# The opening of a hybrid trunk kernel: norm rows spread by TensorE, sample rows in one transfer, bands finished on GpSimd, differences between a group's two weight chunks

## The chip, the cores and the metric

The kernel runs on one core of a Trainium2 chip. The metric is the device time of one execution in microseconds, lower is better. 0.2% of it is 5.0 us.

## What is computed

One step of a two-layer decoder trunk in float32 over 320 tokens (256 of a new prompt, 8 sequences of 8 new tokens each) with 2048 features. Layer 0 mixes by pooling, layer 1 by an mLSTM; a squared-ReLU MLP follows each. The change is in the opening, the pooling mixer of layer 0:

```python
u = rmsnorm(h, norm_mix[layer])
def pool_mixer(u, buf, pos0, w_group, scale):
    u_ext = jnp.concatenate([buf, u], axis=1)          # buf: the last 15 inputs of each sequence
    cs = jnp.cumsum(jnp.pad(u_ext, ((0, 0), (1, 0), (0, 0))), axis=1)
    for g, w in enumerate((2, 4, 8, 16)):              # four groups of 512 features
        s = cs[:, P + 1:P + 1 + T, sl] - cs[:, P + 1 - w:P + 1 - w + T, sl]
        outs.append(s / cnt[None, :, None])            # mean of the last w inputs
    d = (pooled - u_ext[:, P:]).reshape(B, T, 4, 512)
    y = jnp.einsum('btgc,gcd->btgd', d, w_group) * scale
    new_buf = u_ext[:, T:]
h = h + y
h = h + sq_relu_mlp(rmsnorm(h, norm_ffn[layer]), ...)
```

## The kernel before

**The main loops.** Activations lie with features on the partitions and the 320 tokens as columns (hT is the residual, 16 tiles of 128 features). A float32 product is made of three faster ones: operand and weight are each split into a high part (`w_hi`, `a_hi`, `op_hi`, copies by ScalarE, ACT) and a low part (`w_lo`, `a_lo`, `op_lo`, by VectorE, DVE), and TensorE (PE) adds hi·hi, lo·hi and hi·lo in the accumulator G (L1600 to L1602). Weights come in chunks of 128x1024 (512 KB) through a ring of four buffers. A chunk is 24 matmuls of 320 columns. Eight chunks make a slab of 512 output features; slab 0 is the first of the MLP. After a slab, DVE takes its four tiles out of G (`relu`, L1263) and ACT and GpSimd (POOL) square and split them. Each engine has its own queue of instructions, in the order of the code, with waits on semaphores.

**The opening.** Rows of x lie with tokens on the partitions in `xrow` (two prompt tiles of 128, and a tile of 64 sample rows followed by the young state rows). ACT squares and sums each row (L869, one instruction of 2048 columns), DVE and ACT make 1/rms of it (`rcol`). POOL draws for each group g a matrix `band` (memsets L605 and L607, selects L593 and L622) of 1/w where a token counts; DVE multiplies it by `rcol` and takes the identity off (L1190, L1191, L1185). The samples are scaled by `rcol` and by the norm's row `gain` (L1198; `gain` comes in three transfers of repeated rows, `mix_rows`). Then `differences(g)` is 24 rows of matmul on PE (L1631; each float32 matmul shows as two rows): X = xrow times band is d with features on the partitions. ACT and DVE split X into `a_hi` and `a_lo` (L896, L897, L1212, L1214), and two chunks of the pooling weight (L835 and L1129 split them) give the group's output, which DVE adds to hT (L1251, "the evictions"). Group 3 has extra products with `far` (L1638). The order on PE is differences(0), differences(1), chunks 0 and 1, differences(2), chunks 2 and 3, differences(3), chunks 4 and 5, chunks 6 and 7, then the MLP's slab 0. Between the early pieces PE multiplies the identity (`keep_warm`, L1621), whose output nobody reads.

For the MLP's norm ACT squares each tile of hT into `sqt` (L912), one buffer, and POOL adds it to `acc` (L670), 16 times. PE sums `acc` over partitions in slab 0, DVE makes the reciprocal `rv`.

**POOL's list** is: the four draws; then a block of small constants that the mLSTM needs much later (`one`, `causal`, `causal_s`, `parts`, `seqmask`, `fold`, L628 to L649, and two small transfers, L652 and L653), "the constants block"; then the 16 additions to `acc`; then "the tail", which scales the last 32 prompt rows for the output new_buf (L674, L676, 32x2048 each) and sends them out; then the MLP's part.

## Time and profile before

| | |
|---|---|
| time, median of 3 runs | 2481.77 us (2481.02 to 2482.14) |
| time of the profiled execution | 2481.15 us |
| its span | 2479.4 us |
| mean granted clock of TensorE | 0.995 |
| busy share of PE, DVE, ACT, POOL | 99%, 49%, 37%, 20% |
| first matmul of the pooling weights | 27.16 us |
| first matmul of the MLP | 69.00 us |

The span runs from the first to the last instruction; the execution's time is 1.75 us longer. PE is busy in 99% of it, so only what PE waits for, or does at a low clock, can be won without taking work from it. The opening is the first 69 us.

### The profile page before, as it was taken

What the parts mean: (1) busy time and instruction counts of PE and PEld (TensorE: products, weight loads), DVE (VectorE), ACT (ScalarE), POOL (GpSimd) and SP (SyncE); (2) the same over time, 40 slices, a digit from 0 to 9 for tenths busy, and PEclk for the clock granted to TensorE, in tenths of its full rate; (3) what the DMA queues carried; (4) which work ended last, traced back from release to release, by engine and by line L of the source; (5) the groups of instructions that cost most, each with busy time, mean ns of one, the idle gap of its engine ahead of it and who ended that gap; (6) DMA issues with size and microseconds to landing.
All of it is one profiled execution on the core that took longest, in us unless ns stands there. A gap on an engine that the chain in (4) does not pass through costs nothing.

```text
span 2479.4 us, 43406 instructions
## 1 busy us (share of the span) xinstructions
PE 2452.6 (99%) x16344; PEld 2406.8 (97%) x16344; DVE 1207.4 (49%) x1391; ACT 907.2 (37%) x1075; POOL 488.3 (20%) x612
## 2 busy tenths in 40 slices
PE   8999999999999999999999999999999999999998
PEld 8999999999999999999888889999999999999997
DVE  6644344444444454444478885444344444434444
ACT  5433333233333333333355553333333233333332
POOL 5430022012102332210011122221022003101331
PEclk8999999999999999999999999999999999999999
DMA  7544444455444444555377664444454454444443
GB/s 226 153 147 153 147 150 151 146 152 147 150 151 145 151 148 134 145 145 154 107 231 225 228 208 154 149 148 153 145 151 148 148 152 145 151 150 147 152 146 113
DMA packets 197684, 387.22 MB, mean 156 GB/s; under 512 B 12181, under 2 KB 12181, under 8 KB 197173
## 3 DMA queue, kind: packets, MB, share of 16 engines
q1 hardware_dynamic: 197228, 385.46, 49.9%
q0 software_dynamic: 384, 0.78, 0.2%
q8 instruction: 48, 0.79, 0.1%
q14 instruction: 24, 0.20, 0.0%
HBM read 364.01 MB, written 22.64 MB: 156 GB/s over the span
## 4 chain that ended last, share of the span: by engine, by line
PE 95%; DVE 3%; DMA 1%; ACT 0%; issue 0%; SPq 0%; POOL 0%; DVEq 0%; ACTq 0%; POOLq 0%
PE G L1600 30%; PE G L1601 29%; PE G L1602 29%; PE X L1869 1%; PE X L1832 1%; DMA w_raw<-in_pool_w 1%; DVE w_lo L1129 0%; PE X L1631 0%; DMA w_raw<-in_mlstm_w_out 0%; DVE cst L1517 0%; PE X L1876 0%; DVE qkv L1410 0%; PE G L1910 0%; PE G L1912 0%; PE G L1914 0%
## 5 line engine op out<-in xcount | busy, mean ns | idle before, releaser
L1129 DVE TENSOR_TENSOR w_lo<-w_raw,w_hi 128x1024 fp32r<-128x1024 f32 x648 | 833.4, 1288 | 1175.0 <-ACT w_hi L821 1164.5
L821 ACT ACTIVATE w_hi<-w_raw 128x1024 fp32r<-128x1024 f32 x608 | 645.2, 1062 | 1306.2 <-PE G L1602 1275.4
L1600 PE MATMUL G<-op_hi,w_hi 128*128 128x320 f32 x2816 | 876.1, 311 | 0.7 <-DVE qkv L1319 0.7
L1602 PE MATMUL G<-op_hi,w_lo 128*128 128x320 f32 x2816 | 870.8, 309 | 0.0
L1601 PE MATMUL G<-op_lo,w_hi 128*128 128x320 f32 x2816 | 870.7, 309 | 0.0
L1600 PE MATMUL G<-a_hi,w_hi 128*128 128x320 f32 x2304 | 714.6, 310 | 4.3 <-DVE hT L1251 2.7
L1601 PE MATMUL G<-a_lo,w_hi 128*128 128x320 f32 x2304 | 713.6, 310 | 0.0
L1602 PE MATMUL G<-a_hi,w_lo 128*128 128x320 f32 x2304 | 713.4, 310 | 0.0
L1600 PEld LDWEIGHTS G<-op_hi,w_hi 128*128 128x128 f32 x2816 | 529.0, 188 | 8.2 <-issue 5.7
L1601 PEld LDWEIGHTS G<-op_lo,w_hi 128*128 128x128 f32 x2816 | 529.1, 188 | 2.4 <-issue 1.0
L1602 PEld LDWEIGHTS G<-op_hi,w_lo 128*128 128x128 f32 x2816 | 529.1, 188 | 0.0
L1600 PEld LDWEIGHTS G<-a_hi,w_hi 128*128 128x128 f32 x2304 | 433.7, 188 | 5.0 <-issue 3.3
L1601 PEld LDWEIGHTS G<-a_lo,w_hi 128*128 128x128 f32 x2304 | 433.7, 188 | 0.1
L1602 PEld LDWEIGHTS G<-a_hi,w_lo 128*128 128x128 f32 x2304 | 433.6, 188 | 0.0
L693 POOL TENSOR_TENSOR sq<-relu 128x320 f32<-128x320 f32 x128 | 120.7, 943 | 1268.4 <-DVE relu L1263 1268.3
L696 POOL TENSOR_TENSOR a_lo<-sq,a_hi 128x320 f32 x128 | 144.7, 1130 | 25.9 <-POOL sq L693 19.6
L662 POOL TENSOR_TENSOR sqt<-hT 128x320 f32<-128x320 f32 x44 | 44.4, 1008 | 178.1 <-DVE hT L1280 116.2
L918 ACT ACTIVATE a_hi<-relu 128x320 f32 (+1 forms) x128 | 55.5, 473 | 59.7 <-DVE relu L1263 59.3
L1263 DVE SCALAR_TENSOR_TENSOR relu<-G,Rb 128x320 f32<-128x320 f32 x128 | 56.6, 485 | 1.8 <-PE G L1602 1.8
L829 ACT ACTIVATE w_hi<-w_raw 128x1024 fp32r<-128x1024 f32 x32 | 33.9, 1059 | 60.8 <-DMA w_raw<-in_mlstm_w_in 32.8
L664 POOL TENSOR_TENSOR acc<-acc,sqt 128x320 f32<-128x320 f32 x44 | 50.3, 1143 | 3.5
L1271 DVE TENSOR_TENSOR hT<-G,hT 128x320 f32 x96 | 42.5, 485 | 3.0
(284 smaller groups left out, 1034.5 us busy)
## 6 DMA issues: line engine op xcount, KB each, us to landing
w_raw<-in_ffn_w_up SPq DMA_DIRECT2D x256, 512.0 KB, 3.7
w_raw<-in_ffn_w_down SPq DMA_DIRECT2D x256, 512.0 KB, 3.7
w_raw<-in_mlstm_w_in SPq DMA_DIRECT2D x96, 512.0 KB, 3.9
w_raw<-in_mlstm_w_out SPq DMA_DIRECT2D x32, 512.0 KB, 4.5
cst<-in_state_mlstm_C SPq DMA_DIRECT2D x24, 512.0 KB, 4.0
out_C_sample<-cst SPq DMA_DIRECT2D x24, 512.0 KB, 3.1
w_raw<-in_pool_w SPq DMA_DIRECT2D x8, 512.0 KB, 12.1
w_raw<-in_state_mlstm_C SPq DMA_DIRECT2D x8, 512.0 KB, 3.9
```

The costliest lines, as they stand in the source:

```text
L662: pool.tensor_tensor(sqt[:, :], hT[:, k, :], hT[:, k, :], ALU.mult).then_inc(sq_ok, 1)
L664: pool.tensor_tensor(acc[:, :], acc[:, :], sqt[:, :], ALU.add).then_inc(ssq_ok, 1)
L693: pool.tensor_tensor(sq[:, m % 2], relu[:, m], relu[:, m], ALU.mult).then_inc(a_sq_ok, 1)
L696: pool.tensor_tensor(lo, sq[:, m % 2:m % 2 + 1], hi.bitcast(F32), ALU.subtract).then_inc(a_lo_ok, 1)
L821: act.activation(w_hi[:, c % RING], w_raw[:, c % RING], ACT.Copy).then_inc(w_hi_ok, 1)
L918: act.activation(a_hi[:, bass.ds(k0 + m, 1), :], relu[:, m:m + 1], ACT.Square).then_inc(a_hi_ok, 1)
L1129: v.tensor_tensor(w_lo[:, slot], w_raw[:, slot], w_hi[:, slot].bitcast(F32), ALU.subtract).then_inc(w_lo_ok, 1)
L1263: v.scalar_tensor_tensor(out=relu[:, m], in0=G[:, m, 0:T], scalar=0.0, in1=Rb[:, :], op0=ALU.max, op1=ALU.mult).then_inc(evicted, 1)
L1271: v.tensor_tensor(h, G[:, m:m + 1, 0:T], h, ALU.add).then_inc(evicted, 1)
L1600: pe.matmul(G[:, m, 0:T], w_hi[:, slot, t, w], hi[:, k, :], start=first and t == 0, stop=False)
L1601: pe.matmul(G[:, m, 0:T], w_hi[:, slot, t, w], lo[:, k, :], start=False, stop=False)
L1602: ins = pe.matmul(G[:, m, 0:T], w_lo[:, slot, t, w], hi[:, k, :], start=False, stop=last and t == CK - 1)
```

## The change

- **Norm row.** One row of 8 KB is fetched first. PE multiplies a column of ones with it, four matmuls of 512 columns with one row of contraction, into G; DVE copies G to `gain` (four copies of 128x512). The three transfers of `mix_rows` (768 KB) are gone.
- **Samples and young state.** One transfer of 120 rows (`sample_rows`) takes the place of three. The MLP's residual tiles `hT` come in between the pooling chunks.
- **Row sums.** ACT squares half the columns of each tile, DVE the other half (`half_square`).
- **Bands.** POOL takes the identity off while it draws, and multiplies the bands by `rcol` and scales the samples itself for groups 1 to 3 (`rooted`). DVE does so for group 0 only. `idr` is gone.
- **PE's order.** Group 0 is prompt tile 0, prompt tile 1, samples, each with `keep_warm` ahead; all samples' columns of a group's four tiles lie side by side in X, so ACT and DVE split them in one instruction. differences(g+1) stand between chunks 2g and 2g+1, for differences(1) after chunk 0. A group's tiles are made in the order 1, 0, 2, 3, and its first chunk waits for the first two only.
- **Evictions** (`pooled`) on DVE stand after the other work of the next group's turn; 12 of the 16 `op_lo` move behind the group's loop, 10 of them into slab 0.
- **Squares for the norm** go to a ring of six buffers. POOL's 16 additions come right after the bands, the constants block after them, and the tail after that.

The diff, cut to its core:

```diff
-WARM = (10, 5, 10)
+WARM = (8, 4, 6, 6)
+TURN = (1, 0, 2, 3)
+SQ_RING = 6
...
+            sp.dma_start(gain[0:1, :], A["norm_mix"][0:1, :]).then_inc(mix_in, 16)
             for t in range(TT):
-                src = A["x_prompt"][0, t * P:(t + 1) * P, :] if t < 2 else A["x_sample"].rearrange("b t d -> (b t) d")
-                sp.dma_start(xrow[0:ROWS[t], t, :], src).then_inc(x_in[t], 16)
-            gain_load(0, slice(0, NS), parts[0])
...
+                own = band[0:NS, g, BS:BP]
+                link(pool.tensor_tensor(own, own, ident[0:NS, 0:NS], ALU.subtract))
+                two = band[:, g, 0:2 * BT].rearrange("p (a n) -> p a n", n=BT)[:, :, 0:P]
+                pool.tensor_tensor(two, two, bc(ident[:, :], [P, 2, P]), ALU.subtract).then_inc(band_drawn, 1)
...
+            def rooted(g):
+
+                for t in range(2):
+                    at = slice((B0, B1)[t], (B1, BS)[t])
+                    pool.wait_ge(r0_ok, t + 1)
+                    pool.tensor_scalar(band[:, g, at], band[:, g, at], rcol[:, t:t + 1], None, ALU.mult).then_inc(band_ok, 1)
+                    pool.wait_ge(band_ok, 2 * (g - 1) + t + 1)
+                pool.wait_ge(r0_ok, 3)
+                x = xrow[0:NS, 2, g * NC:(g + 1) * NC]
+                link(pool.tensor_scalar(x, x, rcol[0:NS, 2:3], None, ALU.mult))
+                pool.wait_ge(gain_ok, g + 1)
+                pool.tensor_tensor(x, x, gain[0:NS, g * NC:(g + 1) * NC], ALU.mult).then_inc(u_ok, 1)
+                pool.wait_ge(u_ok, g)
+
+            draw(0)
+            for g in range(1, GROUPS):
+                draw(g)
+                rooted(g)
+            link(pool.memset(acc[:, :], 0.0))
+            for k in range(KT):
+                pool.wait_ge(sq_ok, k + 1)
+                pool.tensor_tensor(acc[:, :], acc[:, :], sq0(k), ALU.add).then_inc(ssq_ok, 1)
+                pool.wait_ge(ssq_ok, k + 1)
             link(pool.memset(causal[:, :], 0.0))
             select(causal[:, :], [[1, P]], -1, fill=NEG)
...
             x = xrow[P - GP:P, 1, :]
             pool.wait_ge(d_ok, KT)
             link(pool.tensor_scalar(x, x, rcol[P - GP:P, 1:2], None, ALU.mult))
-            pool.wait_ge(gain_in[2], 16)
+            pool.wait_ge(gain_ok, GROUPS)
             pool.tensor_tensor(x, x, gain[P - GP:P, :], ALU.mult).then_inc(tail_ok, 1)
             pool.wait_ge(tail_ok, 1)
-            pool.wait_ge(u_ok, GROUPS)
...
             square(0)
             tile_root(0)
             square(1)
+            tile_root(1)
             square(2)
-            tile_root(1)
+            act.wait_ge(vecs_in, 16)
+            d_hi(0, 1)
             tile_root(2)
-            act.wait_ge(vecs_in, 16)
             split_pool(0)
+            for i in TURN[1:]:
+                d_hi(0, i)
             split_pool(1)
-
...
+            for g in range(GROUPS + 1):
+                if g < GROUPS:
+                    for n in (2 * g + 2, 2 * g + 3):
+                        split_pool(n) if n < 8 else split(0, n - 8)
+                else:
+                    split(0, LEAD - 1)
+                done = range(MT * (g - 1), MT * g) if g else ()
+                for k in done:
                     act.wait_ge(evicted, k + 1)
                     op_split(0, k, vec(V_FFN + k))
-                    if k:
-                        act.wait_ge(ssq_ok, k)
-                    act.activation(sqt[:, :], hT[:, k, :], ACT.Square).then_inc(sq_ok, 1)
+                if g + 1 < GROUPS:
+                    for i in TURN:
+                        d_hi(g + 1, i)
+                for k in done:
+                    if k >= SQ_RING:
+                        act.wait_ge(ssq_ok, k - SQ_RING + 1)
+                    act.activation(sq0(k), hT[:, k, :], ACT.Square).then_inc(sq_ok, 1)
 
...
+            def half_square(t):
+
+                v.wait_ge(x_in[t], 16)
+                if t:
+                    v.wait_ge(x_sqv, t)
+                x = xrow[0:ROWS[t], t, D // 2:]
+                v.scalar_tensor_tensor(out=junk[0:ROWS[t], D // 2:], in0=x, scalar=1.0 / D, in1=x, op0=ALU.mult, op1=ALU.mult,
+                                       accum_out=scol[0:ROWS[t], t:t + 1]).then_inc(x_sqv, 1)
...
+            for g in range(3):
+                gain_of(g)
+            half_square(0)
+            gain_of(3)
+            tile_inverse(0)
             v.wait_ge(band_drawn, 1)
-            band_of(0, 2)
-            tile_inverse(0)
...
+            d_lo(0, 1)
             split_pool(0)
-            d_lo(0)
+            for i in TURN[1:]:
+                d_lo(0, i)
             split_pool(1)
...
+            for g in range(GROUPS):
+                if g:
+                    pooled(g - 1)
+                split_pool(2 * g + 2) if g < GROUPS - 1 else split(0, 0)
+                if g + 1 < GROUPS:
+                    for i in TURN:
+                        d_lo(g + 1, i)
+                split_pool(2 * g + 3) if g < GROUPS - 1 else split(0, 1)
+                if g:
+                    op_split(0, g - 1, V_FFN)
+            pooled(GROUPS - 1)
+            op_split(0, GROUPS - 1, V_FFN)
+            split(0, LEAD - 1)
+            for k in (4, 5):
...
+            pe.wait_ge(mix_in, 16)
+            for g in range(GROUPS):
+                pe.matmul(G[:, g, :], one[0:1, 0:1].broadcast_to([1, P]), gain[0:1, g * NC:(g + 1) * NC], start=True,
+                          stop=True).then_inc(gain_sum, 1)
+            pe.wait_ge(gain_ok, 1)
+            keep_warm(WARM[0])
             pe.wait_ge(x_in[0], 16)
...
+            for i in (1, 2, 3, 0):
+                ins = prompt(0, i, 1)
+                if i:
+                    ins.then_inc(d_ok, 1)
+            keep_warm(WARM[2])
             pe.wait_ge(x_in[2], 16)
-            keep_warm(WARM[2])
-            pe.wait_ge(band_ok, 3)
...
                 for c in range(2):
                     n = 2 * g + c
+                    pe.wait_ge(d_lo_ok, MT * g + (4 if c else 2))
                     pe.wait_ge(w_lo_ok, n + 1)
                     free = (lambda m: pe.wait_ge(evicted, MT * (g - 1) + m + 1)) if g and c == 0 else None
                     chunk(n % RING, a_hi, a_lo, 4 * g + CK * c, c == 0, c == 1, free)
+                    if c == 0 and g + 1 < GROUPS:
+                        differences(g + 1)
```

DVE's list opens like this before (`idr` is identity times `rcol`, `w_lo` the low part of the first chunk):

```order
L1185 TENSOR_TENSOR band<-band,ident 64x64 [waits band_drawn,idr_set,consts]
L1176 TENSOR_SCALAR rcol<-xcol 128x1 [waits x_sq]
L1178 RECIPROCAL rcol<-rcol 128x1 [waits r0_inv]
L1190 TENSOR_SCALAR idr<-ident,rcol 128x128 [waits r0_ok]
L1191 SCALAR_TENSOR_TENSOR band<-band,rcol,idr 128x144 [waits dve_chain]
...
L1198 SCALAR_TENSOR_TENSOR xrow<-xrow,rcol,gain 64x512 [waits gain_in0,r0_ok]
...
L1129 TENSOR_TENSOR w_lo<-w_raw,w_hi 128x1024 [waits w_hi_ok,vecs_in]
```

and like this in the changed kernel (`gain_sum` is counted by the four spreading matmuls, `x_sqv` by DVE's own squares):

```order
L1204 COPY gain<-G 128x512 [waits gain_sum,consts]
L1204 COPY gain<-G 128x512 [waits gain_sum] x2
L1212 SCALAR_TENSOR_TENSOR junk,scol<-xrow 128x1024 [waits x_in0]
L1204 COPY gain<-G 128x512 [waits gain_sum]
L1221 SCALAR_TENSOR_TENSOR rcol<-xcol,scol 128x1 [waits x_sqv,x_sq]
L1224 RECIPROCAL rcol<-rcol 128x1 [waits r0_inv]
L1230 TENSOR_SCALAR band<-band,rcol 128x144 [waits r0_ok,band_drawn]
L1212 SCALAR_TENSOR_TENSOR junk,scol<-xrow 128x1024 [waits x_sqv,x_in1]
...
L1263 SCALAR_TENSOR_TENSOR xrow<-xrow,rcol,gain 64x512 [waits gain_ok,r0_ok]
L1235 SCALAR_TENSOR_TENSOR a_lo<-X,vecs,a_hi 128x256 [waits d_hi_ok,vecs_in]
L1158 TENSOR_TENSOR w_lo<-w_raw,w_hi 128x1024 [waits w_hi_ok]
```

Three copies and a square of 1024 columns now stand ahead of the first band, and the band no longer goes through `idr`.

PE's list around the first chunk, before (L1600 and L1601 open chunk 0; each row of L1631 is one matmul):

```order
L1631 MATMUL X<-band,xrow 128x128
L1631 MATMUL X<-band,xrow 128x64
L1631 MATMUL X<-band,xrow 128x144 [waits state_in1,d_lo_ok,u_ok,band_ok]
L1631 MATMUL X<-band,xrow 128x128
L1631 MATMUL X<-band,xrow 128x64
...
L1600 MATMUL G<-a_hi,w_hi 128x320 [waits w_lo_ok,d_lo_ok]
L1601 MATMUL G<-a_lo,w_hi 128x320
```

and in the changed kernel (L1668 is `keep_warm`, L1688 the samples, L1680 the prompt part, L1647 to L1649 the chunks):

```order
L1688 MATMUL X<-band,xrow 128x64 [waits u0_ok,x_in2]
L1688 MATMUL X<-band,xrow 128x64 x3
L1668 MATMUL G<-ident 128x128 x6
L1647 MATMUL G<-a_hi,w_hi 128x320 [waits w_lo_ok,d_lo_ok,gain_ok]
L1648 MATMUL G<-a_lo,w_hi 128x320
...
L1680 MATMUL X<-band,xrow 128x144 [waits d_lo_ok,u_ok,band_ok]
...
L1688 MATMUL X<-band,xrow 128x64 x4
...
L1647 MATMUL G<-a_hi,w_hi 128x320 [waits w_lo_ok,d_lo_ok]
```

The 12 matmuls of differences(1) moved from ahead of chunk 0 to behind it.

POOL's list from the last band on, before:

```order
L622 AFFINE_SELECT band<-band 64x64 [waits pool_chain]
L628 MEMSET one 128x1 [waits band_drawn]
L629 MEMSET causal 128x128 [waits pool_chain]
...
L653 DMA m<-in_state_mlstm_m 4x8x1
L667 MEMSET acc 128x320
L670 TENSOR_TENSOR acc<-acc,sqt 128x320 [waits sq_ok,pool_chain]
L670 TENSOR_TENSOR acc<-acc,sqt 128x320 [waits sq_ok,ssq_ok] x15
L674 TENSOR_SCALAR xrow<-xrow,rcol 32x2048 [waits d_ok,ssq_ok]
L676 TENSOR_TENSOR xrow<-xrow,gain 32x2048 [waits gain_in2,pool_chain]
```

and in the changed kernel (L653 adds to `acc`, L655 opens the constants block, L678 and L679 end it, L695 and L697 are the tail):

```order
L643 TENSOR_TENSOR xrow<-xrow,gain 64x512 [waits gain_ok,pool_chain]
L650 MEMSET acc 128x320 [waits u_ok]
L653 TENSOR_TENSOR acc<-acc,junk 128x320 [waits sq_ok,pool_chain]
L653 TENSOR_TENSOR acc<-acc,junk 128x320 [waits sq_ok,ssq_ok] x15
L655 MEMSET causal 128x128 [waits ssq_ok]
...
L678 DMA bgate<-in_mlstm_b_gate 4x2x1 [waits pool_chain]
L679 DMA m<-in_state_mlstm_m 4x8x1
L695 TENSOR_SCALAR xrow<-xrow,rcol 32x2048 [waits d_ok]
L697 TENSOR_TENSOR xrow<-xrow,gain 32x2048 [waits gain_ok,pool_chain]
```

The additions moved ahead of the constants block, and the block now lies between them and the tail.

## Rows read from the trace of the kernel before

**Rows 1.** The page: busy time, share of the span, instructions.

```profile
PE 2452.6 (99%) x16344; PEld 2406.8 (97%) x16344; DVE 1207.4 (49%) x1391; ACT 907.2 (37%) x1075; POOL 488.3 (20%) x612
```

**Rows 2.** PE's timeline, the opening: start, duration, instruction, xcount, [idle before <-releaser].

```profile
1.75 7.22 PE L1621 MATMUL G<-ident 128*128 128x128 f32 x38 [1.75 <-POOL ident L598]
...
21.84 5.56 PE L1631 MATMUL X<-band,xrow 128*128 128x144 f32 x24 [4.99 <-DVE a_lo L1214]
27.16 0.61 PE L1600 MATMUL G<-a_hi,w_hi 128*128 128x320 f32 x1
...
34.57 2.87 PE L1631 MATMUL X<-band,xrow 128*128 128x144 f32 x24
37.25 0.39 PE L1600 MATMUL G<-a_hi,w_hi 128*128 128x320 f32 x1
...
44.37 0.80 PE L1631 MATMUL X<-band,xrow 128*128 128x144 f32 x6
...
49.05 0.42 PE L1600 MATMUL G<-a_hi,w_hi 128*128 128x320 f32 x1
...
59.10 0.60 PE L1600 MATMUL G<-a_hi,w_hi 128*128 128x320 f32 x1 [2.72 <-DVE hT L1251]
...
69.00 0.31 PE L1600 MATMUL G<-op_hi,w_hi 128*128 128x320 f32 x1
```

**Rows 3.** ACT's timeline, the opening and slab 0.

```profile
5.74 1.91 ACT L869 ACTIVATE junk<-xrow 128x2048 f32<-128x2048 f32 x1 [3.44 <-DMA xrow<-in_x_prompt]
...
19.51 1.06 ACT L835 ACTIVATE w_hi<-w_raw 128x1024 fp32r<-128x1024 f32 x1 [4.11 <-DMA w_raw<-in_pool_w]
20.47 0.46 ACT L896 ACTIVATE a_hi<-X,vecs 128x256 fp32r<-128x256 f32 x1
...
83.34 1.06 ACT L821 ACTIVATE w_hi<-w_raw 128x1024 fp32r<-128x1024 f32 x1 [2.46 <-PE G L1602]
```

**Rows 4.** Windows (start:end): duration, busy time by engine, then PEclk, DMA share, GB/s.

```profile
1214.00:1218.50 4.50, 2.08 (x12) 1.01 (x11) 4.37 (x6) 2.80 (x4) 0.00 (x0) 1.00 0.00 0
1219.00:1222.00 3.00, 3.00 (x13) 3.00 (x13) 0.91 (x4) 0.00 (x0) 0.49 (x4) 0.50 0.02 5
```

**Rows 5.** DVE's timeline, the opening.

```profile
14.04 0.73 DVE L1198 SCALAR_TENSOR_TENSOR xrow<-xrow,rcol,gain 64x512 f32<-64x512 f32 x1
...
16.66 1.21 DVE L1129 TENSOR_TENSOR w_lo<-w_raw,w_hi 128x1024 fp32r<-128x1024 f32 x1
```

**Rows 6.** Groups of instructions, 70 to 96 us | busy, mean ns | idle before.

```profile
L670 POOL TENSOR_TENSOR acc<-acc,sqt 128x320 f32<-128x320 f32 x4 | 3.5, 880 | 6.1 <-ACT sqt L912 6.1
L1219 DVE SCALAR_TENSOR_TENSOR op_lo<-hT,vecs,op_hi 128x320 fp32r<-128x320 f32 x4 | 3.3, 840 | 0.8 <-ACT op_hi L889 0.8
```

**Rows 7.** POOL's timeline: the last draw, the constants block, the tail.

```profile
21.37 0.28 POOL L622 TENSOR_SCALAR_AFFINE_SELECT band<-band 64x64 f32<-64x64 f32 x1
...
21.87 0.20 POOL L629 MEMSET causal<- 128x128 f32 x1
...
22.87 4.19 POOL L593 TENSOR_SCALAR_AFFINE_SELECT causal_s<-causal_s 64x64 f32<-64x64 f32 x4
...
35.79 0.64 POOL L653 DMA_DIRECT2D m<-in_state_mlstm_m  x1
...
75.21 7.47 POOL L674 TENSOR_SCALAR xrow<-xrow,rcol 32x2048 f32<-32x2048 f32 x1
82.76 4.89 POOL L676 TENSOR_TENSOR xrow<-xrow,gain 32x2048 f32<-32x2048 f32 x1
```

**Rows 8.** DVE's timeline beside the tail, to the evictions of slab 0.

```profile
75.07 8.09 DVE L1129 TENSOR_TENSOR w_lo<-w_raw,w_hi 128x1024 fp32r<-128x1024 f32 x4 [1.14 <-ACT w_hi L821]
84.44 5.43 DVE L1129 TENSOR_TENSOR w_lo<-w_raw,w_hi 128x1024 fp32r<-128x1024 f32 x2 [1.28 <-ACT w_hi L821]
...
95.53 1.22 DVE L1129 TENSOR_TENSOR w_lo<-w_raw,w_hi 128x1024 fp32r<-128x1024 f32 x1 [1.99 <-ACT w_hi L821]
96.67 1.72 DVE L1263 SCALAR_TENSOR_TENSOR relu<-G,Rb 128x320 f32<-128x320 f32 x4
```

More of the change, by code:

```diff
@@ L302, in build @@
         x_in = [sem(f"x_in{t}") for t in range(TT)]
-        state_in = [sem(f"state_in{i}") for i in range(3)]
-        gain_in = [sem(f"gain_in{i}") for i in range(3)]
+        mix_in = sem("mix_in")
+        far_in = sem("far_in")
+        gain_sum = sem("gain_sum")
+        gain_ok = sem("gain_ok")
         h_in = [sem(f"h_in{g}") for g in range(GROUPS)]
@@ L600, in _, with draw @@
             pool.wait_ge(consts, 1)
-            for g in range(GROUPS):
+            def draw(g):
                 w = 2 << g
@@ L1194, in samples @@
-            def samples(g):
-                x = xrow[0:NS, 2, g * NC:(g + 1) * NC]
-                v.wait_ge(gain_in[1 if g else 0], 16)
-                v.scalar_tensor_tensor(out=x, in0=x, scalar=rcol[0:NS, 2:3], in1=gain[0:NS, g * NC:(g + 1) * NC],
-                                       op0=ALU.mult, op1=ALU.mult).then_inc(u_ok, 1)
-            def bands(g):
-                v.wait_ge(band_drawn, g + 1)
-                for t in range(TT):
-                    band_of(g, t)
-                samples(g)
@@ L1295, in ready @@
                     v.wait_ge(r_ok, rj)
-                slab(s0, hidden(s0, f0), {5: norm, 7: ready})
+                slab(s0, hidden(s0, f0), {**(more or {}), 5: norm, 7: ready})
                 with v.Fori(1, MT) as j:
@@ L1309, in ffn @@
                     slab(s0 + sl * 8 + j, hidden(s0 + sl * 8 + j, f0 + sl * KT + j * MT))
-            ffn(0, S_FFN0, 1)
+            ffn(0, S_FFN0, 1, {i: op_splits(i) for i in range(5)})
             for j in range(MT):
@@ L1625, in _, with features @@
             keep_warm(9)
[L1627 to L1639 removed]
+            def features(g, i):
+                return slice((MT * g + i) * P, (MT * g + i + 1) * P)
@@ new lines, in prompt, with samples @@
+            def prompt(g, i, t):
+                at, b = ((slice(0, BT), B0), (slice(P, TP), B1))[t]
+                return pe.matmul(X[i][:, at], xrow[:, t, features(g, i)], band[:, g, b:b + at.stop - at.start], start=t == 0,
+                                 stop=t == 1, skip_group_check=True)
+            def samples(g):
+                rows = NS + NSEQ * NEAR
+                for i in range(MT):
+                    at = slice(TP + i * NS, TP + (i + 1) * NS)
+                    ins = pe.matmul(X[0][:, at], xrow[0:rows, 2, features(g, i)], band[0:rows, g, BS:BP], start=False,
+                                    stop=g < GROUPS - 1, skip_group_check=True)
+                    if g == GROUPS - 1:
+                        ins = pe.matmul(X[0][:, at], far[0:NS, i * P:(i + 1) * P], band[0:NS, g, BP:BP + NS], start=False,
+                                        stop=True, skip_group_check=True)
@@ L1665, in _ @@
-            for i in range(MT):
-                of_tile(0, i, 1)
-                last_tile(0, i)
+            pe.wait_ge(x_in[1], 16)
+            pe.wait_ge(band0_ok, 2)
+            for i in (1, 2, 3, 0):
+                ins = prompt(0, i, 1)
+                if i:
+                    ins.then_inc(d_ok, 1)
+            keep_warm(WARM[2])
+            pe.wait_ge(x_in[2], 16)
+            pe.wait_ge(u0_ok, 1)
+            samples(0)
+            keep_warm(WARM[3])
+            pe.wait_ge(gain_ok, GROUPS)
```

198 lines of the change are left out of this document (82 added, 116 removed).

## The prediction, made before the changed kernel ran

> **What bounds the kernel now.** I read the page first: PE is busy for 2452.6 us, 99% of the span [rows 1], so a change can give back only the remaining 27 us of idle time and what a low clock costs. Then PE's timeline up to the first matmul of the MLP at 69.00 [rows 2], because the diff touches nothing else on PE. The reader is to see three things there. The first chunk begins at 27.16. From there PE works, apart from one wait of 2.72 us ahead of chunk 6, on the evictions. And the work itself should take less than the 41.84 us that it takes: a chunk lasts 3.52 us (ACT's split of a slab's chunk takes 1.06 and idles 2.46 for the next one, which PE sets [rows 3]), eight are 28.2, differences(2) is 2.7 (34.57 to 37.25), differences(3) 4.7 (44.37 to 49.05), the wait 2.7, together 38.3. The missing 3.5 us are the clock. After the wait, chunks 6 and 7 take 9.90 us (59.10 to 69.00) for 7.04, so 2.9 are lost there; differences(1) shows the same, 5.56 us for the 24 rows that take 2.87 later [rows 2], the clock at 1.2 GHz instead of 2.4, and the start at 27.16 has some of it.
>
> What held the first chunk was ACT's order: it waited 4.11 us for the second weight chunk at 19.51 before it split the first X at 20.47 [rows 3], and differences(1) stood ahead of chunk 0.
>
> **The start S of chunk 0 after the change.** The warm-up rows give the clock's two speeds: 38 rows in 7.22 us [rows 2], 0.21 us each at the start. A spreading matmul has 512 columns for their 128, two rows, so 4 x 2 x 0.21 = 1.7 us at half speed and 0.87 at full. Nine warm-ups end at 1.75 + 18 x 0.21 = 5.6, three spreads at about 9.1. DVE's copies of 512 columns are not in the trace; the samples' product of 512 columns takes 0.73, a `w_lo` of 1024 columns 1.21 [rows 5], half of it 0.6: I take 0.65. So the copies end at 9.8, x has been there since 5.74 [rows 3], and DVE's half square (1.2, as a 1024-column `w_lo`) ends at 11.0, the fourth copy at 11.7, the inverse, root and band by my estimate 1.1 later at 12.8 (short instructions; before, from the end of ACT's square at 7.65 the same steps and one more needed 1.4, until PE's first product, whose warm-ups end at 8.97 [rows 2, 3]). ACT's half square (half of 1.91) is hidden behind it. Each further tile costs DVE 1.2 + 0.9: 14.9 and 16.9, then the samples' scaling 0.73: 17.6. PE's sample matmuls, ACT's two splits and DVE's two (0.46 each, as at 20.47 [rows 3]) follow: 20.2. DVE's nine instructions in this chain that read two SBUF operands stand beside POOL, which draws without pause. What that costs: four selects of the block took 4.19 us from 22.87 on, beside DVE's splits and band products, where a lone one of the same size took 0.28 [rows 7]. In this direction POOL pays; the other is seen in the tail. Bounds 0 and 3 us, taken 1.5, since POOL's pieces here are short. **S = 21.7**, between 20.2 and 23.2, for 27.16.
>
> **From S to the MLP.** Eight chunks 28.2, differences(1) at full speed 2.7, differences(2) 2.7, differences(3) 4.7: 38.3.
> Waits: before, differences(2) and (3) stood between the groups and hid the evictions; now each group's first chunk follows the last chunk of the one before at once. After the last matmul of differences(g+1), ACT splits (0.46), DVE splits (as much), makes a `w_lo` (1.21), an `op_lo` (0.84 [rows 6]) and the first eviction (about 0.45, as the four `relu` in 1.72 [rows 8]); with some 0.4 of hand-overs 3.8 us, against 3.52 of PE's chunk beside them. So at least 0.3 at three places; with one of POOL's 0.88 additions [rows 6] let in between, 1.2 or more. Taken 2.5 for the three (bounds 0.9 and 4.5). The 2.72 wait goes, as the MLP's first two splits no longer stand ahead of that eviction.
> Clock: a drop costs 2.9, as after 59.10. There is one more in the middle of the kernel: PE was busy for 2.08 of the 4.50 us to 1218.50, and then ran at 0.50 [rows 4]. The new waits, about 1 us each, are shorter than both, but the opening has gaps of 1 to 2 us as well, close behind each other. I take 3.5 as before (bounds 0 and 7).
> The MLP begins at F = 21.7 + 38.3 + 2.5 + 3.5 = 66.0, **3.0 us earlier**.
>
> The Trainium skill ("TensorE: Matmul & The Clock Gate", Why this matters for your kernels) warns only of idle gaps between bursts longer than any here, the 2.72 included. The trace has the drop after 2.72 us [rows 2], so it is stricter than the page. By the page the 3.5 would be nothing; that is rival A.
>
> **The tail.** POOL used to finish the constants block at 36.4 (21.87 to 36.43, 14.6 us [rows 7]), long ahead of the tail at 75.21, which was F + 6.2. Now the block comes behind the additions, which end about F + 7.5, so the tail starts at F + 22 to F + 25. While L674 ran, DVE's four `w_lo` took 8.09 us for 4 x 1.15; while L676 ran, two took 5.43 for 2.3 [rows 8]: one is held up 3.5, the other 3.1. Before, ACT's next split was 2 to 3 us away, so that cost nothing. Now DVE's last two `w_lo` ahead of slab 0's evictions fall there: the last was at 95.53, F + 26.5, and the one before it a chunk earlier, F + 23, and the evictions began at 96.67, F + 27.7 [rows 8]. Slab 1 needs the first at F + 28.4 (8 x 3.52 and 0.3 for the norm's sum), 0.3 after its end. With the first tail instruction from F + 23, the last `w_lo` ends 0.7 to 2.5 us late. Taken **1.1 us lost**, bounds 0 and 3.7.
> The skill says of such a pair (the page "SBUF — State Buffer", SBUF: two separate sides) that the one that starts first holds the port for its whole instruction. L676 lasted 4.89 us and held a `w_lo` up 3.1, L674 7.47 and 3.5, so the rows are milder; by the page the loss could be 2 us larger, and the time 2481.6.
>
> Hidden: ACT's larger splits, the squares' ring (ACT waits 2.46 us for each chunk as it is), the 10 `op_lo` in slab 0 (two and a `w_lo` are 2.9 us per chunk of 3.52, with three chunks of lead; where they stood before, each would delay an eviction by its 0.84). The DMAs: the first chunk's weights must be there by 18, and 768 KB less stands ahead of them.
>
> **Sum**, against the profiled execution: 2481.15 - 3.0 + 1.1 = 2479.25. That execution lies 0.6 below the median shown, so I add half of it: **2479.6**, within 0.2% (5.0 us, about what a measurement here can tell from no change).
>
> **Rivals.**
> A, the clock holds: S and waits as above, no stretch at half speed from S on and none of the tail's loss. 2479.6 - 3.5 - 1.1 = 2475.0, by 2473 if DVE meets POOL nowhere. For it: the work that waits is short, and PE idles less than before. Against it: 2.72 us sufficed. 0.23.
> B, no gain at all: POOL's longer list (per group two subtractions, three scalings and a product more, some 2.5 us) makes the band of group 3 late, PE waits 1 to 2 us for it in the middle of group 2, the three evictions are late by 1.2 to 1.5, and the clock falls twice. 66.0 + 2.6 puts F at 68.6, the time at 2482.2. For it: in the trace POOL's last band ends at 21.65 already with fewer steps, and its selects stretch beside DVE [rows 7]. 0.18.
> C, slower: L697, not L695, meets the last `w_lo`. That happens if L695 starts between F + 17.6 and F + 21.3. DVE is then held to F + 31, slab 1 waits up to 3.7 and starts at half clock, 2.9 more: 6.6 lost for the 1.1 taken, 2485.1; with B's waits 2487.7, which is more than 5 us slower. For it: additions that end at F + 6 and a block without collisions, 14.6, give F + 20.6. Against it: the block lengthens beside DVE's `op_lo`. 0.12, of it 0.05 beyond +5 us.
> The forecast has 0.47 (its own range 2477.5 to 2482).
>
> **Numbers.** Faster by over 0.2% (below 2476.8) is most of A and a little of the forecast: 0.23. Slower (above 2486.7): C with B, and waits that I have not seen: 0.07. Range: 2474.5 leaves out a third of A, 2485.0 half of C: 2474.5 to 2485.0.
>
> **What the profile would show.** Chunk 0 at 20 to 23; three waits for `evicted` of 0.3 to 1.5 at chunks 2, 4 and 6 in place of the 2.72; the MLP's first matmul at 63 to 68.5; L695 at F + 20 to F + 25 and a DVE `w_lo` stretched beside it; a wait of PE for `relu` at slab 1. The forecast is wrong if S is past 24, if PE waits for bands, or if L697 covers the last `w_lo`.

## The result, and the profile after

The changed kernel takes 2489.84 us (median of 7 runs, 2485.64 to 2491.74), the kernel before 2481.77 (7 runs, 2480.59 to 2483.34): ratio 1.0028, 95% interval 1.0019 to 1.0037, so 8.1 us slower. The forecast was 2479.6 with a range to 2485.0. The profiled execution took 2490.72, its span is 2489.0. All comparisons are between fast runs; one of the 11 runs of before_block below took 8667.88 us and is left out of its figures.

As in the prediction, S is the start of chunk 0 and F the first matmul of the MLP.

PE's timeline of the changed kernel, the rows that answer to [rows 2] (L1668 warm-up, L1711 spreading, L1680 prompt, L1688 samples, L1691 `far`):

```profile
1.91 4.21 PE L1668 MATMUL G<-ident 128*128 128x128 f32 x18 [1.91 <-POOL ident L600]
6.05 7.19 PE L1711 MATMUL G<-gain,one 1*128 1x512 f32 x8
13.17 3.78 PE L1668 MATMUL G<-ident 128*128 128x128 f32 x16
16.75 1.52 PE L1680 MATMUL X<-band,xrow 128*128 128x144 f32 x8
...
23.97 0.38 PE L1647 MATMUL G<-a_hi,w_hi 128*128 128x320 f32 x1 [0.34 <-issue]
27.56 1.10 PE L1680 MATMUL X<-band,xrow 128*128 128x144 f32 x8
...
49.89 1.17 PE L1680 MATMUL X<-band,xrow 128*128 128x144 f32 x8 [2.17 <-issue]
...
68.30 0.31 PE L1647 MATMUL G<-op_hi,w_hi 128*128 128x320 f32 x1
...
100.87 0.64 PE L1647 MATMUL G<-op_hi,w_hi 128*128 128x320 f32 x1 [3.70 <-DVE relu L1310]
```

S is 23.97 for 27.16, so 3.2 us earlier, and F is 68.30 for 69.00, so only 0.7. Between the two PE waits 2.17 us ahead of differences(3), and it waits 3.70 us more ahead of slab 1. Both waits are followed by half speed, in these windows of the changed kernel (columns as in [rows 4]; PEclk is the third number from the end):

```profile
50.00:55.00 5.00, 5.00 (x24) 4.28 (x24) 0.48 (x1) 0.47 (x1) 3.64 (x5) 0.66 0.00 0
55.00:60.00 5.00, 5.00 (x25) 4.88 (x26) 3.43 (x6) 3.86 (x9) 1.67 (x1) 0.65 0.00 0
...
100.00:105.00 5.00, 4.13 (x15) 4.13 (x16) 3.23 (x6) 2.61 (x5) 0.79 (x2) 0.50 0.79 210
```

POOL's timeline names what the first wait was for, and what stood behind it:

```profile
44.82 1.98 POOL L637 TENSOR_SCALAR band<-band,rcol 128x144 f32<-128x144 f32 x2
46.89 1.56 POOL L641 TENSOR_SCALAR xrow<-xrow,rcol 64x512 f32<-64x512 f32 x1
48.53 1.25 POOL L643 TENSOR_TENSOR xrow<-xrow,gain 64x512 f32<-64x512 f32 x1
...
89.18 5.46 POOL L695 TENSOR_SCALAR xrow<-xrow,rcol 32x2048 f32<-32x2048 f32 x1
94.73 4.59 POOL L697 TENSOR_TENSOR xrow<-xrow,gain 32x2048 f32<-32x2048 f32 x1
```

Group 3's samples are scaled at 49.78, and differences(3) begins at 49.89. DVE's timeline, its first square and then the other end:

```profile
12.18 1.22 DVE L1212 SCALAR_TENSOR_TENSOR junk<-xrow 128x1024 f32<-128x1024 f32 x1
...
91.31 2.67 DVE L1158 TENSOR_TENSOR w_lo<-w_raw,w_hi 128x1024 fp32r<-128x1024 f32 x1 [0.24 <-ACT w_hi L843]
94.83 5.58 DVE L1158 TENSOR_TENSOR w_lo<-w_raw,w_hi 128x1024 fp32r<-128x1024 f32 x1 [0.84 <-ACT w_hi L843]
100.33 1.67 DVE L1310 SCALAR_TENSOR_TENSOR relu<-G,Rb 128x320 f32<-128x320 f32 x4
```

L697 began 0.1 us ahead of the last `w_lo`, which took 5.58 us for 1.21; the evictions began 32.0 us after F, for 27.7 before [rows 8]. That is rival C; the tail began at F + 20.9. The wait for group 3 is rival B's. Both happened.

To place the time I compare the same ACT instruction in both traces, the split behind slab 1's start, before:

```profile
101.42 1.06 ACT L821 ACTIVATE w_hi<-w_raw 128x1024 fp32r<-128x1024 f32 x1 [1.57 <-PE G L1602]
```

and after:

```profile
107.10 1.06 ACT L843 ACTIVATE w_hi<-w_raw 128x1024 fp32r<-128x1024 f32 x1 [3.65 <-PE G L1649]
```

5.7 us are lost by there: 0.7 ahead up to the MLP, 6.4 lost at the slab boundary (3.7 of waiting, the rest the clock). The spans differ by 9.6, so 3.9 more were lost far from the change. Windows of the changed kernel:

```profile
1222.50:1229.00 6.50, 6.07 (x18) 3.84 (x19) 3.06 (x5) 0.94 (x1) 0.49 (x4) 0.50 0.01 3
1482.00:1485.00 3.00, 3.00 (x13) 3.00 (x12) 1.66 (x2) 0.13 (x1) 0.00 (x0) 0.50 0.66 206
```

The first stretch is the one that the kernel before has at 1219 to 1222 [rows 4], later by the 5.7 us and longer: 6.8 us at a granted clock of 0.50 for 3.4. The second, 3.4 us long, the kernel before does not have. So the mLSTM in the middle had 10.2 us at half speed for 3.4, which is 3.4 us of lost time, most of the 3.9. Whether that belongs to the change is asked again below.

### The profile page after: what moved, and what is told of

It is laid out like the page before. It is cut to its first block, busy times and chain, and to the rows that moved or that the text cites. A ratio compares the mean times of both kernels' runs of the same rounds, so it can differ in the third digit from the quotient of the medians.

```text
span 2489.0 us, 43425 instructions
## 1 busy us (share of the span) xinstructions
PE 2463.7 (99%) x16350; PEld 2411.6 (97%) x16350; DVE 1208.0 (49%) x1374; ACT 900.9 (36%) x1063; POOL 509.8 (20%) x631
## 4 chain that ended last, share of the span: by engine, by line
PE 95%; DVE 2%; DMA 1%; issue 1%; ACT 0%; SPq 0%; DVEq 0%; POOL 0%; ACTq 0%; POOLq 0%
PE G L1647 29%; PE G L1649 29%; PE G L1648 29%; PE X L1933 1%; PE X L1896 1%; DMA w_raw<-in_mlstm_w_out 0%; PE G L1668 0%; PE X L1940 0%; DMA w_raw<-in_mlstm_w_in 0%; DVE cst L1564 0%; DVE qkv L1457 0%; DVE w_lo L1158 0%; PE X L1680 0%; PE G L1974 0%; PE G L1978 0%
## 5 line engine op out<-in xcount | busy, mean ns | idle before, releaser
L1647 PE MATMUL G<-op_hi,w_hi 128*128 128x320 f32 x2816 | 878.3, 312 | 4.4 <-DVE relu L1310 3.7
L1649 PE MATMUL G<-op_hi,w_lo 128*128 128x320 f32 x2816 | 872.5, 310 | 0.0
L1647 PE MATMUL G<-a_hi,w_hi 128*128 128x320 f32 x2304 | 714.1, 310 | 2.8 <-DVE a_lo L1469 2.1
L1649 PE MATMUL G<-a_hi,w_lo 128*128 128x320 f32 x2304 | 713.2, 310 | 0.0
L1647 PEld LDWEIGHTS G<-op_hi,w_hi 128*128 128x128 f32 x2816 | 530.1, 188 | 12.6 <-issue 6.1
L1649 PEld LDWEIGHTS G<-op_hi,w_lo 128*128 128x128 f32 x2816 | 530.2, 188 | 0.0
L1647 PEld LDWEIGHTS G<-a_hi,w_hi 128*128 128x128 f32 x2304 | 433.4, 188 | 3.7 <-DVE w_lo L1158 2.5
L1649 PEld LDWEIGHTS G<-a_hi,w_lo 128*128 128x128 f32 x2304 | 433.4, 188 | 0.0
L718 POOL TENSOR_TENSOR a_lo<-sq,a_hi 128x320 f32 x128 | 143.9, 1124 | 25.8 <-POOL sq L715 19.6
```

The source lines that it names most:

```text
L718: pool.tensor_tensor(lo, sq[:, m % 2:m % 2 + 1], hi.bitcast(F32), ALU.subtract).then_inc(a_lo_ok, 1)
L1647: pe.matmul(G[:, m, 0:T], w_hi[:, slot, t, w], hi[:, k, :], start=first and t == 0, stop=False)
L1649: ins = pe.matmul(G[:, m, 0:T], w_lo[:, slot, t, w], hi[:, k, :], start=False, stop=last and t == CK - 1)
```

## The experiments

Theory T: two independent losses, POOL late with group 3, and the tail's second instruction in front of DVE's last `w_lo`. "Opening" below is the offset of the ACT split just shown against the first profile of before, so it leaves out the middle of the kernel. One thing varies in it that no edit touched: in the ten profiles that have the spreading matmuls, the eight rows took 7.19 us in six, and 3.86 to 4.49 in four (tail_first, no_tail, pieces_again, after_early), and S came 2.4 to 2.8 us earlier (in the first three, where the code ahead of it is the same). So what an edit behind S is worth is better read from S or from F on: from F to that ACT split the kernel before takes 32.4 us and the changed kernel 38.8. Ratios are to the kernel before, run on the same chip.

**tail_first.** In the changed kernel, the constants block behind the tail:

```diff
-            link(pool.memset(causal[:, :], 0.0))
...
             x = xrow[P - GP:P, 1, :]
...
             pool.dma_start(O["pool_new"], xrow[0:NS, 2, :]).then_inc(pool_out, 16)
+            link(pool.memset(causal[:, :], 0.0))
...
```

> The changed kernel with POOL's constants block moved behind the tail; nothing else. Theory T (the loss at the slab boundary is the tail's second instruction, 4.6 us, in front of DVE's last w_lo of slab 0): the tail begins near the end of the additions, F + 7 to F + 8, the wait of PE ahead of slab 1 (3.7 us) and the low clock behind it (2.7 us) go, and the median falls by about 6, to 2483 to 2485. Rival R (DVE is late because ten op_lo were put into slab 0): the wait stays, and the median stays at 2488 to 2491.

2487.26 us, ratio 1.0020 (1.0010 to 1.0029), above the expected 2483 to 2485. Half right. The wait at slab 1 is gone, but a new one of 2.60 us stands in the middle of slab 0. Rows of PE, POOL and DVE:

```profile
21.14 0.39 PE L1648 MATMUL G<-a_hi,w_hi 128*128 128x320 f32 x1 [0.34 <-issue]
...
83.35 0.64 PE L1648 MATMUL G<-op_hi,w_hi 128*128 128x320 f32 x1 [2.60 <-DVE op_lo L1245]
```

```profile
72.72 5.57 POOL L670 TENSOR_SCALAR xrow<-xrow,rcol 32x2048 f32<-32x2048 f32 x1
78.38 4.57 POOL L672 TENSOR_TENSOR xrow<-xrow,gain 32x2048 f32<-32x2048 f32 x1
```

```profile
71.81 5.10 DVE L1245 SCALAR_TENSOR_TENSOR op_lo<-hT,vecs,op_hi 128x320 fp32r<-128x320 f32 x2
76.83 1.21 DVE L1159 TENSOR_TENSOR w_lo<-w_raw,w_hi 128x1024 fp32r<-128x1024 f32 x1
77.96 5.33 DVE L1245 SCALAR_TENSOR_TENSOR op_lo<-hT,vecs,op_hi 128x320 fp32r<-128x320 f32 x2
```

Two `op_lo`, 1.0 us a pair elsewhere, took 5.1 and 5.3 beside the tail's two instructions. The ten `op_lo` in slab 0, which the prediction called hidden with three chunks of lead, have room for one such hold but not for two. Opening +1.5, so 4.2 better than the changed kernel; but 2.8 of that is S, 21.14 for 23.97, which this edit does not touch. From F on it takes 37.4 us for 38.8, so in this profile the edit won 1.4; the medians have it at 3.1, each with an interval of some 2 us to either side.

One more thing is seen here: with S at 21.14 PE still waits 2.17 us ahead of differences(3), at 47.11, and POOL is done with group 3's samples at 47.01, 2.8 us earlier, as S is. So that wait does not come from a late S.

**dve_samples.** The samples' scaling of groups 1 to 3 back on DVE:

```diff
-                link(pool.tensor_scalar(x, x, rcol[0:NS, 2:3], None, ALU.mult))
-                pool.tensor_tensor(x, x, gain[0:NS, g * NC:(g + 1) * NC], ALU.mult).then_inc(u_ok, 1)
+                v.scalar_tensor_tensor(out=x, in0=x, scalar=rcol[0:NS, 2:3], in1=gain[0:NS, g * NC:(g + 1) * NC], op0=ALU.mult,
+                                       op1=ALU.mult).then_inc(u_ok, 1)      # samples(1) ahead of split_pool(1), then one a group
```

> The changed kernel with the samples' scaling of groups 1 to 3 back on DVE (one instruction of 0.73 us each in place of two of POOL that took 3.3 us together). Theory T (PE's wait in the middle of group 2 is POOL, late with group 3): POOL has group 3 some 10 us earlier, the wait of 2.2 us and the low clock behind it (3.4 us) go, F falls from 68.3 to 62.5 to 64; the wait at slab 1 stays, since the tail still comes behind the block. Median 2483 to 2486. Rival R (the wait there is of the clock or of DVE's splits, POOL only ends at the same time): F stays at 67 to 69, median 2488 to 2490.

2484.78 us, ratio 1.0004 (0.9995 to 1.0013). Right in the mechanism and the median, not in F: POOL's group 3 is ready at 40.7, nothing waits ahead of differences(3), the MLP begins at 65.47 (expected 62.5 to 64); the wait at slab 1 is 3.7 us as before. POOL, dve_samples:

```profile
39.37 1.35 POOL L637 TENSOR_SCALAR band<-band,rcol 128x144 f32<-128x144 f32 x2
```

The MLP is 2.8 us earlier, not the 4 to 6 that I expected, since two waits for evictions came up in place (1.17 and 1.14 us), which DVE's 0.74 more per group and the end of POOL's delay explain by my reading.

**both_edits.**

> Both edits together. Theory T: the two losses are independent, 5.6 and 6.4 us, so the median is 2477 to 2479, faster than the kernel before. If one loss only hid the other, it stays within 2 us of the better of the two single edits, 2482 to 2484.

2480.83 us, ratio 0.9991 (0.9982 to 1.0000). Against the median of before on its own chip the changed kernel is at +8.1, tail_first at +5.0, dve_samples at +2.5, this one at -1.5: the single edits give 3.1 and 5.6, both 9.6, so within the noise they add, and neither loss hid the other. It is above the expected 2477 to 2479 by what tail_first showed, the tail among the `op_lo` (again one wait, 2.61 us).

**before_block.** The kernel before, with only the constants block moved between the additions and the tail:

```diff
+            link(pool.memset(acc[:, :], 0.0))          # and the 16 additions
             link(pool.memset(causal[:, :], 0.0))       # the constants block
...
-            link(pool.memset(acc[:, :], 0.0))
             x = xrow[P - GP:P, 1, :]                   # the tail
```

> The kernel before with one thing changed: the constants block moved from ahead of the 16 additions to between them and the tail, as in the changed kernel. Theory T: the tail starts at F + 20 to F + 23 instead of F + 6.2, its second instruction stands in front of the w_lo at F + 26.5, PE waits 2 to 4 us for the evictions and is slow behind them: median 2485 to 2488. Rival R (DVE late by its own op_lo, which this kernel has not in slab 0): 2481 to 2483, no difference.

2486.5 us, ratio 1.0017 (1.0008 to 1.0027), 4.2 us slower. Right, and the clearest single proof: one block moved, and the kernel before loses at the same place. It is not quite without `op_lo` in slab 0, as the expectation has it (see [rows 6]), but its four end at 73.7, 15 us ahead of the tail. In this profile the 3.0 us of waiting were all of it: the clock behind them stayed at 1.00, and the opening is +2.8. Its POOL, DVE and PE rows:

```profile
94.23 4.61 POOL L676 TENSOR_TENSOR xrow<-xrow,gain 32x2048 f32<-32x2048 f32 x1
```

```profile
95.00 4.92 DVE L1129 TENSOR_TENSOR w_lo<-w_raw,w_hi 128x1024 fp32r<-128x1024 f32 x1 [1.52 <-ACT w_hi L821]
```

```profile
100.38 0.42 PE L1600 MATMUL G<-op_hi,w_hi 128*128 128x320 f32 x1 [3.04 <-DVE relu L1263]
```

**no_tail.** dve_samples without the tail's two instructions, so new_buf leaves out their scaling:

```diff
-            link(pool.tensor_scalar(x, x, rcol[P - GP:P, 1:2], None, ALU.mult))
-            pool.tensor_tensor(x, x, gain[P - GP:P, :], ALU.mult).then_inc(tail_ok, 1)
+            pool.memset(x[:, 0:1], 0.0).then_inc(tail_ok, 1)
```

> The kernel with the samples' scaling on DVE (dve_samples), and the two instructions of the tail left out, so that the prompt's new_buf is written without its scaling; the constants block stays where the change put it. Theory T (the tail's length on the port is all that is wrong behind F): the wait ahead of slab 1 (3.7 us) and its low clock (2.6 us) go, nothing takes their place. Opening ahead of before by 3 to 4 us, median 2478 to 2480. Rival R (DVE is late in slab 0 by its ten op_lo and the block's 20 small selects): PE still waits 1 us or more somewhere in slab 0, median 2481 to 2484.

2477.71 us, ratio 0.9980 (0.9971 to 0.9989). Right. Against dve_samples the tail's 10 us on POOL cost 7.9 by the medians (+2.5 and -5.4 to before), and 6.3 in the profiles from F on: 32.4 us, as before, for 38.7. All ten `op_lo` are still in slab 0 here, so they cost nothing by themselves.

**pieces.** dve_samples with the tail in eight pieces:

```diff
+            tails = [(q, half) for q in range(GROUPS) for half in range(2)]
+            def tail():
+                q, half = tails.pop(0)
+                x = xrow[P - GP:P, 1, q * NC:(q + 1) * NC]      # scaled by rcol, then by gain
...
                 link(pool.memset(parts[rows, (n + 1) % 4, :], 0.0))
+                tail()                                          # one piece after every few selects
```

> dve_samples with the tail cut into eight pieces of 512 columns (about 1.2 us each), one after every few selects of the constants block; same work, same place in POOL's list as a whole. Theory T: no DVE instruction is held up more than 1.2 us, DVE has three chunks of lead in slab 0, so it costs nothing: like no_tail, median 2478 to 2480.5. Rival R (what counts is the sum of what POOL takes from DVE, not the length of a piece): 7 us of port time among DVE's op_lo are as bad as before, PE waits 2 to 3 us in slab 0 as in both_edits, median 2480.5 to 2483.

2478.18 us, ratio 0.9982 (0.9973 to 0.9991). Right: POOL does the same work, in pieces of 1.3 to 2.7 us, but the last `w_lo` ahead of the evictions is not held up, and from F on it takes 32.4 us, as before and as without the tail. DVE, pieces:

```profile
91.83 1.23 DVE L1165 TENSOR_TENSOR w_lo<-w_raw,w_hi 128x1024 fp32r<-128x1024 f32 x1 [2.29 <-ACT w_hi L850]
92.98 1.72 DVE L1327 SCALAR_TENSOR_TENSOR relu<-G,Rb 128x320 f32<-128x320 f32 x4
```

**pieces_early** and **after_early.** Squares and bands ahead of three of DVE's copies, an earlier root, 6 warm-ups for 24, on pieces and on the changed kernel:

```diff
-WARM = (8, 4, 6, 6)
+WARM = (0, 0, 0, 6)
-            for g in range(3):
-                gain_of(g)
+            gain_of(0)
             half_square(0)
...
-            d_hi(0, 1)
             tile_root(2)
+            d_hi(0, 1)
```

> pieces, with DVE's squares and bands ahead of the copies of the norm row for groups 1 to 3, the samples' root on ACT ahead of the first X split, and 6 warm-up matmuls instead of 24 behind the spreading ones. Theory T (S = 24.0 was set by the spreading matmuls, 1.8 us each, and by DVE's copies waiting for them): S falls to 20.5 to 22.5, median 2475 to 2478. Rival R (PE needs the warm-ups, the first chunk runs at a low clock): S falls but 2 to 3 us are lost behind it, median 2478 to 2481.

> The changed kernel with only the early edits of pieces_early. Theory T (POOL's band and samples of group 3 set the middle of group 2, whatever S is): S falls by 1.5 to 3.5 us, PE's wait inside group 2 grows by nearly as much, F stays within 1 us of 68.3, median 2488 to 2491. Rival R (all of POOL's list moves with S, since it waited for rcol too): F and the median fall by 2 us or more, 2486 to 2488.

pieces_early: 2478.87 us, ratio 0.9985 (0.9976 to 0.9994). S fell to 20.34 and the MLP to 61.43, the opening is 7.6 ahead of before, the best of all; but the median is no better than that of pieces and lies where the rival had it. The rival's reason is not seen: the first chunk's rows took 0.31 us, as at full speed. The profile lost 4.9 in the middle of the kernel, which may hide the gain in the median; that was not settled. after_early: 2485.61 us, ratio 1.0009 (1.0000 to 1.0018), and there my theory failed and the rival was right. PE's wait for group 3 did not grow, it vanished (MLP at 63.33). POOL waits for `rcol` three times in `rooted(1)` of the changed kernel, 4.6 us in all, and here for none, so its list moved with the squares: group 3's samples were ready at 46.24 for 49.78. And PE came later behind S, at S + 25.0 for S + 23.8, after a wait of 0.59 and a first chunk that began at half speed, so that it met POOL at 46.35. The 3.7 us at slab 1 stayed.

**mix_dma.** pieces with the spreading undone:

```diff
-            sp.dma_start(gain[0:1, :], A["norm_mix"][0:1, :]).then_inc(mix_in, 16)
+            sp.dma_start(gain[0:NS, 0:NC], A["mix_rows"][0:NS, 0:NC]).then_inc(gain_in[0], 16)     # behind the samples
+            sp.dma_start(gain[0:NS, NC:D], A["mix_rows"][0:NS, NC:D]).then_inc(gain_in[1], 16)     # behind chunk 1
+            sp.dma_start(gain[P - GP:P, :], A["mix_rows"][P - GP:P, :]).then_inc(gain_in[2], 16)   # behind hT
-                pe.matmul(G[:, g, :], one[0:1, 0:1].broadcast_to([1, P]), ...)
```

> pieces with the norm row's spreading undone: no one-row matmuls and no copies, but the repeated rows of the norm fetched by DMA again (768 KB in three transfers, two of them among the pooling chunks). Theory T (S was set by the spreading matmuls and DVE's copies behind them): DVE begins its square at 5.8 instead of 12.2, S comes to 17 to 19.5 for 23.9, the opening gains 4 to 6 us on pieces, less what a later weight chunk costs; median 2474 to 2477. Rival R (the weights or POOL's bands then bind: 768 KB are 2.2 us of DMA): S at 20 or later, or a wait inside groups 0 or 1, median 2477 to 2479, no gain.

2480.27 us, ratio 0.9989 (0.9980 to 0.9998): the rival was right in the mechanism, though the median lies 1.3 above its range. The first square begins at 5.86 and the first prompt product at 8.72 for 16.75, but the transfers then bind: the samples' square waits 2.56 us for its rows, S is 20.46, and later a weight chunk is late. ACT and PE, mix_dma:

```profile
34.67 1.06 ACT L864 ACTIVATE w_hi<-w_raw 128x1024 fp32r<-128x1024 f32 x1 [6.40 <-DMA w_raw<-in_pool_w]
```

```profile
44.73 0.60 PE L1656 MATMUL G<-a_hi,w_hi 128*128 128x320 f32 x1 [3.77 <-DVE hT L1285]
```

So the spreading delays the start, and the transfers that it spares make up for that. By the medians pieces, with the spreading, is 2 us ahead (4.9 faster than before for 2.9), which the two intervals do not separate.

**before_again, after_again, pieces_again.** One more profile of each.

> The kernel before, profiled once more. Theory T (the stretches at a low clock in the middle of the kernel, near 1220 us and between 1370 and 1480 us, differ from one execution to the next of the same program): the opening is the same within 1 us up to the MLP, and the middle costs 0 to 5 us more or less than in the first profile. Rival R (they belong to the program): the profile repeats the one stretch near 1219 us and no other.

> The changed kernel, profiled once more. Theory T: PE's wait for group 3's band and the one ahead of slab 1 come again, 2 to 4 us each; the low clock behind them may be of another length, and the first chunk starts at 24 or, where the spreading matmuls ran at full clock, at 21.5. Rival R: all stretches repeat as in the first profile.

> pieces, profiled once more. Theory T: no wait of PE over 1.3 us in the opening or slab 0; the middle of the kernel may differ from the first profile by up to 5 us. Rival R: it repeats the single stretch near 1372 us.

2484.15, 2491.20 and 2477.95 us, one run each. The two waits of the changed kernel came again (2.9 and 3.7 us, opening +6.7), pieces had none over 1.3. From F on after_again takes 37.8 us, 5.3 more than before for the first profile's 6.4. The middle of the kernel before was not as in its first profile. Its windows:

```profile
1218.80:1222.00 3.20, 3.20 (x10) 1.69 (x9) 2.02 (x4) 0.00 (x0) 0.49 (x4) 0.50 0.00 0
1379.20:1382.40 3.20, 3.20 (x13) 3.11 (x12) 2.85 (x6) 3.12 (x6) 0.00 (x0) 0.50 0.93 243
68.50:71.70 3.20, 3.20 (x13) 3.20 (x13) 3.02 (x6) 2.04 (x5) 1.75 (x2) 0.50 0.80 293
```

A second stretch at half speed at 1379 made the middle 2.1 us longer, in the same program. pieces_again had its extra stretches elsewhere than pieces.

The opening of the kernel before was not the same either. Its 2.71 us ahead of chunk 6 came again, but the clock stayed at 1.00 behind them, and PE then waited for DVE's `w_lo` ahead of the MLP:

```profile
59.01 0.39 PE L1600 MATMUL G<-a_hi,w_hi 128*128 128x320 f32 x1 [2.71 <-DVE hT L1251]
...
68.31 0.52 PE L1600 MATMUL G<-op_hi,w_hi 128*128 128x320 f32 x1 [2.02 <-DVE w_lo L1129]
```

before_block did the same (2.72, then 2.04 and F at 68.40). So the 2.9 us that the low clock took after 59.10 in the first profile had brought F only 0.7 later: DVE would have held PE anyway.

## Why the prediction was wrong

The failed steps in short: the start of the tail at "F + 22 to F + 25", measured F + 20.9, which brought 6.4 us lost for the 1.1 taken; POOL's list, which stands in no term of the sum, and for which PE waited 2.17 us; and the three spreads, which took 5.4 us for the 3.4 of the sum, so that S came 2.3 late.

- **What bounds the kernel now**: right. All that the change won or lost in the opening was in PE's waits and in the clock behind them.
- **S**: 21.7 with 20.2 to 23.2, measured 23.97, outside. The step that failed is "1.7 us at half speed and 0.87 at full" and "three spreads at about 9.1". I let the clock rise at about 7.2, as before; all four spreads ran at half speed (7.19 us), and the square waited until 12.18, where the sum has 9.8. In pieces_again they ran at full speed and S was 21.57, in no_tail 21.47, in tail_first 21.14, so the forecast of S fits those executions, and both profiles of the changed kernel have the slow spreads. What decides between the two was not found. The copies (0.69 for 0.65) and each further tile's 2.1 (2.2) were right. The 1.5 us for DVE beside POOL are not seen in this chain: DVE's squares took 1.22 and the samples' scaling 0.74. In their place DVE waited 1.42 us for ACT's root of the samples' tile.
- **From S to the MLP**: 38.3 of work, nearly right (39.0 in dve_samples, 41.3 less its two waits). "Taken 2.5 for the three" evictions: the changed kernel had none over 0.3, the repaired ones 0.7 to 1.2 at one or two places. The wait that came instead was rival B's. The step that failed is the one that is missing from the sum: I costed POOL's longer list at 2.5 us a group as a rival and gave it no term, where the pair on 64x512 alone took 2.8 to 3.6 a group. POOL was done with group 3 at S + 25.8, PE was there at S + 23.8. The place (ahead of differences(3)) and the size (1 to 2, measured 2.17) were nearly as rival B had them. With S at 21.14 the wait was the same 2.17 (tail_first), so it is not the late S that made it.
- **Clock**: 3.5, measured 3.1 behind the wait at 49.89 (18.4 us to 68.30 for differences(3) and three chunks, 15.3). Right in size by luck, since it followed a wait that the sum does not have. And "3.5 as before" leans on one profile: in the other two that have the 2.7 us wait of before, before_again and before_block, the clock did not fall behind it. Rival A did not occur.
- **The tail**: mechanism and place were right. What failed is "so the tail starts at F + 22 to F + 25": the additions ended at F + 7.1 and the block took 13.7 us, for the 14.6 of [rows 7], so L695 began at F + 20.9, inside C's "between F + 17.6 and F + 21.3". I had the block stretch beside DVE's `op_lo`; it did not. C's price was 6.6, measured 6.4 and, in after_again, 5.3.
- **The chances**: B had 0.18 and C 0.12, of it 0.05 for both together, "with B's waits 2487.7". Both came, in both profiles. They are two separate losses: dve_samples takes away B's wait and keeps the 3.69 us at slab 1, and the two edits add. The measured time lies 2.1 above even the sum of both.
- **What no rival had**: the middle of the kernel. It differs between executions of one program, by 2.1 us between the two profiles of before. In the twelve profiles of changed or edited kernels it was 2.7 us longer on average than in the first profile of before (-0.4 to 5.4). So the first profile of before was a good one, and of the 8.1 us the opening explains 5.7 to 6.7, or 4.8 to 5.8 against the second profile of before. Whether the changed kernel's middle is longer by more than chance stays open.

The Trainium skill's rule that GpSimd and VectorE share a port and that the one that starts first holds it for the whole instruction (the page "SBUF — State Buffer", SBUF: two separate sides) was here nearer than I made it for L697: its 4.59 us held the last `w_lo` up 4.4 (5.58 less 1.21). I had read L676 as milder, 3.1 for its 4.89 us [rows 7, 8]; but that `w_lo` came at 84.44, and L676 ended at 87.65, 3.2 later, so it was held to the end there too. For the other instruction of the tail the traces do not agree with the rule: L695 ran from 89.18 to 94.64, and the `w_lo` beside it, held 1.5 us, was done at 93.98. In tail_first L670 ran from 72.72 to 78.29, and a `w_lo` took its plain 1.21 us at 76.83. In both, DVE went on some 3.6 us after the start of this instruction, an estimate from these rows.

## What to carry to other kernels

Before an instruction of several microseconds on GpSimd is moved, find what VectorE does where it lands: 10 us of work that cost nothing at one place cost 5.3 to 6.4 at another, and nothing again in eight pieces at the same place. When a block is moved from ahead of an instruction to behind it, the instruction behind the block moves too; compute its new start with the block's measured length (here 14.6, later 13.7), and if the range of that start touches the range that is costly (here 3.7 us wide and 0.7 away from the forecast's), price it in the sum and not as a rival. Give every engine whose list the change makes longer a term of its own. And before two profiles are compared, see whether a part that neither edit touched ran the same in both: here S alone moved by 2.8 us.
